# Expert matrices one at a time in four places, and the order of the first weight pieces

## The reference, cut to what matters

```python
N_GROUPS = 4; EXPERTS_PER_GROUP = 8; N_EXPERTS = 32; TOP_K = 2; EXPERT_HIDDEN = 512
...
x = x + mix
hf = rms_norm(x, ffn_norm_w[i])
# every token picks one group, then two experts in it; weights w = softmax(top 2) * group probability
...
hid = jax.nn.silu(xblk @ w_gate[e]) * (xblk @ w_up[e])      # 2048 -> 512, twice
y[token] += (hid @ w_down[e]) * w                           # 512 -> 2048
...
return rms_norm(x + y, final_norm_w)
```

## Time and profile before

| | us |
|---|---|
| median of 3 runs (lowest, highest) | 1804.15 (1799.27, 1805.01) |
| the profiled execution: its time | 1804.94 |
| its span, first to last instruction | 1803.0 |

### The profile page before, as it was taken

How to read it: one execution, slowest core, us unless ns; L and a number is a source line. 1 busy time by engine, 2 the same in 40 slices (tenths; PEclk the granted TensorE clock), 3 DMA queues, 4 the chain that set the end, 5 groups by cost and what they waited for, 6 DMA issues and landing times.

```text
span 1803.0 us, 24278 instructions
## 1 busy us (share of the span) xinstructions
PE 1371.2 (76%) x10914; PEld 838.8 (47%) x10914; DVE 532.4 (30%) x690; ACT 371.3 (21%) x422; POOL 37.9 (2%) x34
## 2 busy tenths in 40 slices
PE   7999999999999999997558465574564755756654
PEld 7999998455756778875213122131121211311211
DVE  5555444536346376544002010020010100201102
ACT  5444344333132154444001000010000000100001
POOL 1000000001101110000000000000000000000000
PEclk9999999999999999998878787787786887877877
DMA  9554466331111167564899999999999999999993
GB/s 354 206 184 152 139 232 221 106 105 55 55 54 60 37 231 261 211 256 187 365 425 429 429 424 427 425 428 429 425 430 426 429 427 426 427 430 425 430 424 151
DMA packets 94333, 529.06 MB, mean 293 GB/s; under 512 B 7696, under 2 KB 10010, under 8 KB 64698
## 3 DMA queue, kind: packets, MB, share of 16 engines
q1 hardware_dynamic: 89424, 514.50, 70.4%
q0 software_dynamic: 2192, 9.29, 1.4%
q10 hardware_dynamic: 2650, 4.26, 0.6%
HBM read 521.74 MB, written 6.29 MB: 293 GB/s over the span
## 4 chain that ended last, share of the span: by engine, by line
PE 52%; DMA 39%; DVE 4%; ACT 2%; issue 1%; SPq 1%; ACTq 0%; DVEq 0%; POOL 0%; POOLq 0%
DMA arena<-in_expert_w_up 26%; DMA arena<-in_expert_w_down 13%; PE ps L543 11%; PE ps L884 10%; PE ps L991 8%; PE ps L619 5%; PE ps L601 4%; PE ps L1019 3%; PE ps L774 1%; PE ps L505 1%; PE ps L791 1%; PE ps L588 1%; PE ps L793 1%; DVE arena L1578 1%; PE ps L577 1%
## 5 line engine op out<-in xcount | busy, mean ns | idle before, releaser
L991 PE MATMUL ps<-ring,arena 128*32 128x512 f32 x1024 | 276.0, 701 | 129.8 <-DMA arena<-in_expert_w_up 129.8
L991 PE MATMUL ps<-arena 128*32 128x512 f32 x1024 | 275.9, 700 | 88.4 <-DMA ring<-in_expert_w_gate 88.4
L1019 PE MATMUL ps<-arena 128*32 128x512 f32 x512 | 145.8, 728 | 61.0 <-DMA ring<-in_expert_w_down 61.0
L1019 PE MATMUL ps<-ring,arena 128*32 128x512 f32 x512 | 145.8, 728 | 58.7 <-DMA arena<-in_expert_w_down 58.7
L991 PEld LDWEIGHTS ps<-ring,arena 128*32 128x32 f32 x1024 | 64.1, 126 | 233.4 <-DMA arena<-in_expert_w_up 138.4
L543 PE MATMUL ps<-h_hi,w_hi 128*128 128x256 f32 x544 | 154.8, 285 | 4.4 <-DVE w_lo L1450 4.4
L543 PE MATMUL ps<-h_hi,w_lo 128*128 128x256 f32 x544 | 154.6, 284 | 0.0
L543 PE MATMUL ps<-h_lo,w_hi 128*128 128x256 f32 x544 | 154.6, 284 | 0.0
L991 PEld LDWEIGHTS ps<-arena 128*32 128x32 f32 x1024 | 64.7, 126 | 179.6 <-issue 179.0
L619 PE MATMUL ps<-ring,arena 128*128 128x512 f32 x320 | 147.8, 605 | 0.0
L1850 DVE TENSOR_TENSOR arena<-arena,ps 128x512 f32<-128x512 f32 x64 | 44.0, 687 | 319.0 <-PE ps L1029 319.0
(11 more groups left out here) (297 smaller groups left out, 2046.3 us busy)
## 6 DMA issues: line engine op xcount, KB each, us to landing
ring<-in_w_in SPq DMA_DIRECT2D x34, 2048.0 KB, 7.8
ring<-in_expert_w_up SPq DMA_DIRECT2D x16, 4096.0 KB, 21.0
arena<-in_expert_w_up SPq DMA_DIRECT2D x16, 4096.0 KB, 30.3
arena<-in_expert_w_gate SPq DMA_DIRECT2D x15, 4096.0 KB, 20.6
ring<-in_expert_w_gate SPq DMA_DIRECT2D x15, 4096.0 KB, 29.8
arena<-in_expert_w_down SPq DMA_DIRECT2D x8, 4096.0 KB, 20.0
ring<-in_expert_w_down SPq DMA_DIRECT2D x8, 4096.0 KB, 29.3
ring<-in_expert_w_down SPq DMA_DIRECT2D x16, 2048.0 KB, 20.5
```

What stands on the lines that cost most here:

```text
L991: last = mm(ps[32 * j:32 * j + 32, u % 2, :], XS[:, k, 32 * j:32 * j + 32], place(u, j)[:, HID * kk:HID * kk + HID], start=k == 0, stop=k ...
L1019: last = mm(ps[32 * j:32 * j + 32, 2 + nb, :], HIDT[:, kh, 32 * j:32 * j + 32], place(u, j)[:, 2048 * r + 512 * nb:2048 * r + 512 * nb + 512],
```

## The change

The start is reordered: ScalarE and VectorE split the first z pieces before the blocks 4 to 7 of h, and the copy of `rbc` moves behind piece 0 (and to another PSUM bank). In the expert stage one matrix of one expert is loaded at a time, 4 MB in one transfer, into one of four places; only the last matrix of a round goes in two halves. A matrix is loaded when the one four before it has been used. TensorE works on one expert at a time: gate and up products put four groups of 4 k-rows side by side in the array's columns (`up_rows`), and a multiplication with a new constant `fold` sums the four and transposes them. The way back to the tokens (`scatter`) is now done once an expert, with four matmuls of 32 rows at four row positions, and VectorE adds 8 blocks once an expert. The first and last round are written out of the loop. FW has a buffer of its own and is loaded after the router's logits. The end is cut in pieces of 512 and 1024 columns.

The diff at its core; removed lines of the expert loops are left out where "..." stands, since the functions above show them:

```diff
-            pool.wait_ge(S("unit_used"), UPG * GROUPS - 2)
+            pool.wait_ge(S("lgT_ps"), 1)
             pool.dma_start(FW, a["final_norm_w"].partition_broadcast(P)).then_inc(S("fw_in"), 16)
...
+        UPG = 3 * GE
+        EW = 2 * SLOT
+        def place(n):
+            p = n % 4
+            if p % 2 == (p > 1):
+                return A(12288 if p else 0, EW)
+            return ring[:, 2:4, :].rearrange("p s n -> p (s n)") if p == 1 else ring[:, 0:2, :].rearrange("p s n -> p (s n)")
...
-            def half_unit(u, h, first):
-                src = (eu if u % 2 else eg) if u < 4 else ed
-                sp.dma_start(pair(u, h), src[:, bass.ds(first, 2), SLOT * (u // 2 % 2):SLOT * (u // 2 % 2) + SLOT])\
-                    .then_inc(S(f"unit_full{u % 2}"), 16)
...
+            def uload(i, expert):
+                w = (eg, eu, ed)[i % 3][:, bass.ds(expert, 1), :].rearrange("p e n -> p (e n)")
+                if i == UPG - 1:
+                    sp.dma_start(place(i)[:, 0:SLOT], w[:, 0:SLOT]).then_inc(S("place3"), 16)
+                    sp.dma_start(place(i)[:, SLOT:EW], w[:, SLOT:EW]).then_inc(S("last_half"), 16)
...
+                    sp.dma_start(place(i), w).then_inc(S(f"place{i % 4}"), 16)
...
-            half_unit(1, 0, 0)
+            uload(2, 0)
             sp.wait_ge(S("v_used"), UM + UO)
-            half_unit(1, 1, 2)
-            for u in range(2, UPG):
-                sp.wait_ge(S("unit_used"), u - 1)
-                uload(u, (0, 2))
+            uload(3, 1)
+            for i in range(4, UPG):
+                sp.wait_ge(S("unit_used"), i - 3)
+                uload(i, i // 3)
...
+            for n in range(2 * TT):
+                t, h = divmod(n, 2)
+                sp.wait_ge(S("fin"), n + 1)
+                sp.dma_start(out[0].rearrange("(a p) d -> p a d", p=P)[:, t, 1024 * h:1024 * h + 1024],
+                             fout[:, t, 1024 * h:1024 * h + 1024]).then_inc(S("stored"), 16)
...
+            def scatter(t, banks):
+                for nb in range(4):
+                    last = mm(ps[:, banks[nb], :], CTB[32 * nb:32 * nb + 32, 128 * t:128 * t + 128], YS[32 * nb:32 * nb + 32, :],
+                              start=True, stop=True, tile_position=(32 * nb, 0))
+                last.then_inc(S("scatter_ps"), 1)
+            def up_rows(bank, j, w, i):
+                for c in range(4):
+                    k = 4 * i + c
+                    last = mm(ps[32 * c:32 * c + 32, bank, :], XS[:, k, 32 * j:32 * j + 32], w[:, HID * k:HID * k + HID],
+                              start=i == 0, stop=i == 3, tile_position=(0, 32 * c))
+                return last
+            def experts(g, first, last_group):
...
+                if not first:
+                    pe.wait_ge(S("adds_done"), g * 8 - 2)
+                for q in range(4):
+                    gather(q)
+                for j in range(GE):
+                    new = first and j == 0
+                    def landed(i):
+                        pe.wait_ge(S(f"place{i % 4}"), g * 48 + (16 * (i // 4 + 1) + (16 if i % 4 < 2 else 0)))
+                    landed(3 * j)
...
+                        last = up_rows(0, j, place(3 * j), i)
...
+                        pe.wait_ge(S("ys_done"), g * 4 + j)
+                        pe.wait_ge(S("xs_done"), g * 4 + 4)
+                        if not (first and j == 1):
+                            pe.wait_ge(S("adds_done"), g * 8 + (2 * j - 2))
+                        scatter(0, (4, 5, 6, 7))
+                    landed(3 * j + 1)
...
+                        last = up_rows(1, j, place(3 * j + 1), i)
+                    last.then_inc(S("unit_used"), 1)
+                    if not new:
+                        pe.wait_ge(S("adds_done"), g * 8 + (2 * j - 1))
+                        scatter(1, (4, 5, 6, 7))
+                        pe.wait_ge(S("hid_done"), g * 4 + j)
+                    pe.wait_ge(S("ohw_done"), g * 4 + (j + 1))
+                    for t in range(TT):
+                        last = tp(ps[:, 3, 128 * t:128 * t + 128], OHW[:, 128 * t:128 * t + 128])
+                    last.then_inc(S("ct_ps"), 1)
+                    pe.wait_ge(S("ct_done"), g * 4 + (j + 1))
+                    pe.wait_ge(S("gc_done"), g * 4 + (j + 1))
+                    pe.wait_ge(S("uc_done"), g * 4 + (j + 1))
+                    for m, src in enumerate((GC, UC)):
+                        for k in range(4):
+                            last = mm(ps[:, 3, 128 * m + 32 * k:128 * m + 32 * k + 32],
+                                      src.rearrange("s (m k) -> s k m", k=4)[:, k, :], C("fold"), start=True, stop=True)
+                    last.then_inc(S("fold_ps"), 1)
+                    pe.wait_ge(S("hid_done"), g * 4 + (j + 1))
+                    if not new:
+                        pe.wait_ge(S("ys_done"), g * 4 + j)
+                    landed(3 * j + 2)
...
+                        if j == GE - 1 and k == 2:
+                            pe.wait_ge(S("last_half"), g * 16 + 16)
+                        for nb in range(4):
+                            last = mm(ps[32 * nb:32 * nb + 32, 2, :], HIDT[:, 32 * k:32 * k + 32],
+                                      place(3 * j + 2)[:, 2048 * k + 512 * nb:2048 * k + 512 * nb + 512],
+                                      start=k == 0, stop=k == 3, tile_position=(0, 32 * nb))
...
+            scatter(0, (4, 5, 6, 7))
+            scatter(1, (0, 1, 2, 3))
...
+            z_hi(0, 0)
+            z_hi(1, 0)
             h_split(4)
             h_split(5)
-            z_hi(0, 0)
+            z_hi(2, 0)
             h_split(6)
             h_split(7)
-            z_hi(1, 0)
-            z_hi(2, 0)
             with act.Fori(0, 2) as i:
...
+                    f(GC, ps[:, 0, :], ACT.Copy).then_inc(S("gc_done"), 1)
+                    act.wait_ge(S("ct_ps"), g * 4 + (j + 1))
+                    f(CTB, ps[:, 3, 0:256], ACT.Copy).then_inc(S("ct_done"), 1)
+                    act.wait_ge(S("fold_ps"), g * 4 + (j + 1))
+                    f(SGT, ps[:, 3, 0:128], ACT.Sigmoid).then_inc(S("sg2_done"), 1)
+                    if last_group and j == GE - 1:
+                        f(rstd[:, 0:2], rstd[:, 0:2], ACT.Sqrt).then_inc(S("sqrt_ready"), 1)
+                    act.wait_ge(S("unit_used"), g * UPG + (3 * j + 3))
+                    f(YS, ps[:, 2, :], ACT.Copy).then_inc(S("ys_done"), 1)
...
+                for n in range(8):
+                    t, nb = divmod(n, 4)
+                    act.wait_ge(S("tail_add"), n + 1)
+                    if n:
+                        act.wait_ge(S("tail_sq"), base + n)
+                    f(junk3, x_sb[:, t, 512 * nb:512 * nb + 512], ACT.Square, accum_out=sspart[:, 4 * t + nb:4 * t + nb + 1])\
+                        .then_inc(S("tail_sq"), 1)
...
-            h_out(4)
-            h_out(5)
-            dve.wait_ge(S("pro_ps"), 3)
-            v.tensor_copy(rbc[:, :], ps[:, 1, 0:TOK]).then_inc(S("pro_dve"), 1)
-            dve.wait_ge(S("pro_dve"), 5)
...
+            z_lo(0, 0)
+            dve.wait_ge(S("pro_ps"), 3)
+            v.tensor_copy(rbc[:, :], ps[:, 3, 0:TOK]).then_inc(S("pro_dve"), 1)
+            dve.wait_ge(S("pro_dve"), 5)
+            h_out(4)
+            z_lo(1, 0)
+            h_out(5)
             h_rest(4)
             h_rest(5)
-            z_lo(0, 0)
+            z_lo(2, 0)
             h_out(6)
             h_out(7)
             h_rest(6)
             h_rest(7)
-            for x in range(1, LAG + 1):
-                z_lo(x, 0)
+            z_lo(3, 0)
...
+                for j in range(GE):
+                    if not (first and j == 0):
+                        dve.wait_ge(S("scatter_ps"), g * 8 + (2 * j - 1))
+                        added(0, (4, 5, 6, 7), "adds_done")
+                    dve.wait_ge(S("unit_used"), g * UPG + (3 * j + 2))
+                    v.tensor_copy(UC, ps[:, 1, :]).then_inc(S("uc_done"), 1)
+                    if not (first and j == 0):
+                        dve.wait_ge(S("scatter_ps"), g * 8 + 2 * j)
+                        added(1, (4, 5, 6, 7), "adds_done")
+                    if j == 1 and not last_group:
+                        one_hots(lambda at: bass.ds(g * GE + (at + GE), GE))
+                    dve.wait_ge(S("sg2_done"), g * 4 + (j + 1))
+                    v.tensor_tensor(HIDT, SGT, ps[:, 3, 0:128], ALU.mult).then_inc(S("silu_done"), 1)
+                    dve.wait_ge(S("silu_done"), g * 4 + (j + 1))
+                    v.tensor_tensor(HIDT, HIDT, ps[:, 3, 128:256], ALU.mult).then_inc(S("hid_done"), 1)
+                    if not (last_group and j == GE - 1):
+                        weighted(lambda at: bass.ds(g * GE + (at + j + 1), 1))
...
+            def last_ms(t):
+                dve.wait_ge(S("tail_sq"), 4 * t + 4)
+                if t == 0:
+                    dve.wait_ge(S("sqrt_ready"), 1)
+                step(v.tensor_reduce(rstd[:, t:t + 1], sspart[:, 4 * t:4 * t + 4], AX.X, ALU.add))
```

(9 more changed lines are left out.)

245 lines of the change are left out of this document (100 added, 145 removed).

## The result

The changed kernel takes **1786.01 us** (median of 5 runs, 1785.23 to 1789.82), the kernel before 1804.15 (median of 5 runs made beside them, 1799.27 to 1805.01). The ratio is **0.9903, 95% interval 0.9890 to 0.9917**: 18.1 us faster. The forecast was 1780.5 with a range of 1772 to 1791. The sign and the range held; 5.5 us of the expected 23.7 did not come.

A forecast was written before the change was run, and what follows sets the result against it. The transfer engines were taken to bound the expert stage. Terms -3.1 + 0.35 - 11.3 - 10.1 = -24.2 us against 1804.94 gave 1780.8, stated as 1780.5 for the median, range 1772 to 1791.

The forecast's parts named there:

- Start, -3.1: Prologue: w_lo of piece 0 comes earlier, so TensorE's first z product starts at about 17.6 us, 3.1 us sooner.
- The start's gain is eaten by piece 3: Prologue, one form of the late-TensorE rival (chance 0.13): a late w_lo of piece 3 costs the start's gain, 3 to 6 us.
- Where the stage begins, +0.35: First gather to first released load: all four gather quarters come first, but only one matrix's 32 records; 0.35 us later.
- Stream, -11.3: Expert stage's loads: FW moved out -2.4, no 8 KB rows -2.5, 32 KB rows -6.4; 11.3 us shorter in sum.
- The 8 KB rows: Expert stream: the slower 8 KB rows of each round's last unit disappear, 8 x 0.31 us, -2.5 us.
- The 32 KB rows: Expert stream: a row costs its bytes plus about 9.6 ns, so 84 matrices at 9.71 for 9.79 us give -6.4 us.
- FW moved ahead of the stream: FW's 1 MB load runs free in the gap ahead of the expert stage, near 832 us; -2.4 us.
- TensorE beside it, hidden: Expert stage: TensorE's work takes 18 to 24 us per expert of 29.1 us, so the transfers stay the bound.
- The end, -10.1: Last landing to the span's end: 21.8 us where 31.9 stood, so -10.1 us, bounds -5 and -12.
- TensorE may still be at the first half: I take 2.5: End, first item: the last half's 16 records after the last landing, 1.7 us or 3.4 at low clock, taken as 2.5.
- TensorE is late: Rival: last expert's chain runs at low clock, or piece 3 eats the start's gain; each 3 to 6 us; chance 0.13.
- TensorE as the bound, +125: Rival in the expert stage: products at low clock throughout, 33 us an expert instead of 29.1, +125 us; chance 0.04.

The follow-up runs named there:

- the two start experiments: The changed kernel with its prologue in the old order: 1787.1 us; the kernel before with only the new prologue: 1800.7 us.
- the added matmuls: The changed kernel with ten unread matmuls of 256 columns ahead of TensorE's wait for the last expert's up matrix: 1782.3 us.
- the other copy order: The changed kernel with GC and UC copied in order k, m, so fold matmuls read 128 columns side by side: 1778.5 us.

## Why the prediction was right, and where it missed

**Start, -3.1: right in place and size, not all kept in every execution.** The piece came at 17.46 (forecast 17.6), the lead stood at 3.0 to 3.5 at 210 us, and the medians of the two start experiments give 1.1 and 4.4. The profiled execution lost 2.5 of it to a clock that fell elsewhere. "The start's gain is eaten by piece 3" did not happen: no wait of TensorE for w_lo stands behind the first. (The costs listed in the forecast add to 23.0 and 27.3 us for pieces 2 and 3, not 23.5 and 27.9; the trace has 23.1 and 27.1.)

**Where the stage begins, +0.35: right.** Gather to first released load took 13.59 us for 13.47, that is +0.1. The forecast took two quarters at 6.41 and two at 3.84; they took 9.97 together.

**Stream, -11.3: measured -12.6, mechanism right, size in part by luck.** The 8 KB rows gave 2.4 (forecast 2.5). The 32 KB rows gave 4.4 (forecast 6.4): the cost of a row was 6.5 ns, not 9.6, from the last step on. FW moved ahead of the stream as forecast (its load stands at 835.43 for 832); its 2.4 was not measured by itself. The rest, 3.4 by subtraction and 5.0 by the rates at equal row length, came from a difference between the two stages that no term had and whose cause is open. It covered what the row term lacked; that the last bytes came at 1757, as forecast, is this surplus against a stage that began 2 us late.

**TensorE beside it, hidden: right**, though each of its sizes was off. The fold took 3.92 us an expert and not 1.9, and the mean down record 901 to 926 ns for 728 before. TensorE was busy 83% of the window from 873 to 1000 us and the stream never stopped. The four row positions ran together (1.14 us for the eight records of a scatter).

**The end, -10.1: measured -3.7, the term that failed.** That is outside the term's own bounds of -5 and -12. The sentence that failed is "TensorE may still be at the first half: I take 2.5". Its last down products ended 9.5 us after the last bytes, 8.7 after the moment at which a wait for them would have ended. Everything behind them was right: from YS' copy (1766.53) to the end of the span are 19.6 us, the sum's terms give 19.3. What the sum left out is the chain that begins one matrix earlier. From the up landing (1748.18) TensorE needs 6.49 + 1.14 + 0.44 + 3.92 us and its waits, 13.3 us, before it can take up a down matrix whose last half lands some 9 us after it. The rival *TensorE is late* named this chain and its 3 to 6 us, with a chance of 0.13; it came about, at 6.4, together with a better stream. Three mis-sized parts make up 6.1 of it: the low clock behind 5 us of idle time (2.85, shown by the added matmuls), the fold's strided weights (1.95, shown by the other copy order) and the low clock in most of the last down products (1.3: 4.95 us for 3.64), whose cause is open. The total lay in the range because the range held this rival; the forecast had given it little weight.

**TensorE as the bound, +125: right to leave small.** Products at the low clock did occur: in this trace 23 sets of up products behind waits of 3.4 to 5 us took 4.95 to 6.54 us, and 17 sets of gate products behind waits of at most 1.9 us took 3.64. An expert still fitted into 29.1 us. The forecast's ground that an engine without idle time keeps the full clock did not hold everywhere, as the last section's window shows.

## What to carry to other kernels

When a stream bounds a stage, cost its end from the last two or three landings, not from the last one: the matrix before the last can have the longer chain, and what is hidden in mid stage at any price (a strided weight load, a cold clock behind a wait) is paid in full there. Where an engine idles for a few us ahead of work on the critical path, a few matmuls that nobody reads are worth trying: of the three places tried the traces show 2.6 us for it at one, 0.7 to 2.9 at the second (the clock fell again behind it) and 0.6 to 1.3 at the third. A transfer should take partitions from both halves. Of two medians 3 us apart on such a kernel, only a row in both traces tells the cause, and a stretch whose clock differs between executions needs more than one trace to compare with.

## What the runs showed of the hardware

Transfers to partitions 0 to 63 and 64 to 127 ran at 211 GB/s with a DMA share of 1.00, those to even and odd partitions at 432. Behind a branch that was not entered stood a table load of 1.28 us, with the same table loaded ahead of it. Writing SBUF in steps of 128 fp32, with PSUM read in order, took ScalarE's copy of 128x512 from 0.60 to 1.05 us and VectorE's from 0.69 to 1.04. A weight load of 128x128 at a stride of 4 fp32 took 328 ns for 191. TensorE paused for 1.99 to 2.77 us at one place in twelve kernels and not in the two with six matmuls more at the start. The granted clock fell not only behind idle time: in the changed kernel it fell in a stretch of matmuls of one and of 64 rows without a gap (two of 1x512 took 2.00 us at 395.84, where two took 1.05 before), and the window behind has the lower level of 1.2 GHz while TensorE was busy throughout, now mostly with 128 rows:

```profile
400.00:405.00 5.00, 5.00 (x12) 3.52 (x11) 1.78 (x5) 3.40 (x6) 0.00 (x0) 0.50 0.00 0
```
